# Halving one weight rounding per boundary and reworking the first tile, the norm offset, the end and one bank in a three-block transformer kernel

## The reference

```python
# first block, twice
x = x + 0.5 * norm(swiglu(norm(x), gate, up, down))           # width 2816
x = x + norm(concat(retention, gated_delta)(norm(x)) @ w_out) # 4 + 4 heads of 128, both directions
x = x + norm(cross_attention(norm(x), norm(mem)) @ xattn_o)   # 4 heads of 256, memory of 256 rows
x = x + 0.5 * norm(swiglu(norm(x), gate, up, down))
# second block, once
h = norm(x)
mixed = gate0 * (mamba2(h) @ w_ssm_out) + gate1 * (dilated_attention(h) @ w_att_out)
x = x + mixed @ w_mix_out
x = x + swiglu(norm(x), gate, up, down)
out = norm(x)

def norm(x, w):  # RMS norm over the 1024 columns
    return x * rsqrt(mean(x * x) + 1e-6) * w
```

## Time and profile before

| | |
|---|---|
| median of 3 runs | 1930.05 us (1928.93 to 1930.11) |
| the profiled execution | 1928.99 us, its span 1927.2 us |
| PE busy | 1910.8 us (99%), 11287 matmuls |
| POOL busy | 1544.8 us (80%) |
| ACT busy | 1087.2 us (56%) |
| DVE busy | 708.3 us (37%) |
| idle time of POOL's subtractions, until ACT's `whi` came | 332.0 us |
| chain that ended last | PE 94%, ACT 3%, DVE 2% |
| mean granted TensorE clock | 0.997 |

### The profile page before, as it was taken

How to read it: one execution, slowest core, us unless ns; L and a number is a source line. 1 busy time by engine, 2 the same in 40 slices (tenths; PEclk the granted TensorE clock), 3 DMA queues, 4 the chain that set the end, 5 groups by cost and what they waited for, 6 DMA issues and landing times.

```text
span 1927.2 us, 28342 instructions
## 1 busy us (share of the span) xinstructions
PE 1910.8 (99%) x11287; PEld 1683.6 (87%) x11287; DVE 708.3 (37%) x1406; ACT 1087.2 (56%) x1458; POOL 1544.8 (80%) x1227
## 2 busy tenths in 40 slices
PE   9999999999999999999999999999999999999998
PEld 7888899988888888889999888888999998888887
DVE  2221767521211222138574231113676632122112
ACT  6645674456644575456734665446666667545443
POOL 6998786666899799979776759997767787888995
PEclk9999999999999999999999999999999999999999
DMA  8554543143655565555323536555443444545552
GB/s 320 191 193 173 203 148 132 49 179 124 221 195 192 183 228 198 189 183 195 134 88 110 193 113 217 182 192 212 152 158 136 153 154 153 178 177 202 197 187 98
DMA packets 48661, 331.50 MB, mean 172 GB/s; under 512 B 5393, under 2 KB 6289, under 8 KB 10514
## 3 DMA queue, kind: packets, MB, share of 16 engines
q1 hardware_dynamic: 44208, 314.61, 45.1%
q10 hardware_dynamic: 4322, 15.09, 2.2%
HBM read 328.63 MB, written 1.05 MB: 171 GB/s over the span
## 4 chain that ended last, share of the span: by engine, by line
PE 94%; ACT 3%; DVE 2%; ACTq 1%; issue 0%; DVEq 0%; DMA 0%
PE bank L1942 20%; PE bank L1911 16%; PE bank L1912 16%; PE bank L1913 16%; PE bank L1946 10%; ACT arena L417 1%; PE bank L2050 1%; PE bank L2074 1%; PE bank L2386 1%; PE bank L2402 1%; PE bank L2016 1%; PE bank L2052 1%; PE bank L2508 1%; PE bank L2647 1%; PE bank L2487 1%
## 5 line engine op out<-in xcount | busy, mean ns | idle before, releaser
L390 POOL TENSOR_TENSOR wlo<-raw,whi 128x512 fp32r<-128x512 f32 x1184 | 1501.8, 1310 | 332.6 <-ACT whi L417 332.0
L417 ACT ACTIVATE whi<-raw 128x2048 fp32r<-128x2048 f32 (+1 forms) x299 | 568.1, 1902 | 192.0 <-PE bank L1913 156.6
L417 ACT ACTIVATE arena<-bank 128x512 f32<-128x512 f32 (+4 forms) x389 | 210.8, 552 | 439.8 <-PE bank L1946 266.4
L1942 PE MATMUL bank<-uT,whi 128*128 128x512 f32 x1632 | 408.2, 392 | 0.0
L1942 PEld LDWEIGHTS bank<-uT,whi 128*128 128x128 f32 x1632 | 296.3, 189 | 55.0
L1946 PEld LDWEIGHTS bank<-uT,wlo 128*128 128x128 f32 x1632 | 222.6, 190 | 15.9
L1946 PE MATMUL bank<-uT,wlo 128*128 128x256 f32 x1632 | 227.5, 282 | 0.0
L1911 PE MATMUL bank<-uT,whi 128*128 128x256 f32 x768 | 222.6, 290 | 0.3 <-DVE memT L1221 0.3
L1912 PE MATMUL bank<-uT,whi 128*128 128x256 f32 x768 | 217.1, 283 | 0.0
L1913 PE MATMUL bank<-uT,wlo 128*128 128x256 f32 x768 | 217.1, 283 | 0.0
L1911 PE MATMUL bank<-whi,uT 128*128 128x512 f32 (+1 forms) x416 | 160.8, 387 | 0.0
(11 more groups left out here) (315 smaller groups left out, 2698.6 us busy)
## 6 DMA issues: line engine op xcount, KB each, us to landing
raw<-in_w SPq DMA_DIRECT2D x295, 1024.0 KB, 4.8
rows<-in_rows ACTq DMA_DIRECT2D x22, 512.0 KB, 4.9
raw<-in_w SPq DMA_DIRECT2D x4, 512.0 KB, 7.2
arena<-in_mem ACTq DMA_DIRECT2D x2, 1024.0 KB, 9.5
x<-in_x SPq DMA_DIRECT2D x2, 512.0 KB, 5.4
out<-x SPq DMA_DIRECT2D x2, 512.0 KB, 2.7
arena<-in_amask ACTq DMA_DIRECT2D x1, 576.0 KB, 6.1
cst<-in_cst SPq DMA_DIRECT2D x1, 468.0 KB, 10.9
```

Source lines behind the costliest of these rows:

```text
L390: r = pool.tensor_tensor(wlo[n % LAND][:, k], raw[n % LAND][:, k], whi[n % RING][:, k].bitcast(F32), ALU.subtract)
L417: return act.activation(o, i, f, **k)
L1942: pe.matmul(both, w[0][:, c], parts[:, :, k, :], start=start and k == 0, stop=False)
```

## The change

Six edits, made together:

- **Half rounding.** In `boundary`, unit B is rounded in two activations of 128x1024, one before `u_hi(1)` and one behind it. `w_hi` is counted up by the second.
- **Norm offset.** The offset sum/n + eps of every pre-norm is made by DVE (`pre_bias`, a tensor_scalar of 128x1) and not by ACT. ACT tells with `pre_sum` that the first half's sum is there and waits for `norm_dve` before the root.
- **First tile.** PE multiplies the cleared tile four more times behind the first two matmuls of unit 0, and twice more ahead of unit 1.
- **Memory bank.** The fourth part of y goes to bank 4 and not to bank 6 again, behind a wait for `m_ready`; ACT and DVE copy it right behind the other three.
- **End.** Tile 0's final scaling is moved up and cut in halves. Tile 1's is shared: POOL multiplies half 0 by the weights and ACT scales it by the reciprocal, DVE does both for half 1. SP stores tile 1 from `ub`.
- **Semaphores.** `cst_in`, `pos_in` and `lvl_in` become one, `tables_in`, waited for at 48; `cleared` becomes `pool_side`.

```diff
@@ -345,17 +345,18 @@
                 if n == 0:
                     sp.dma_start(x[:, 1, :], a["x"][:, 1, :]).then_inc(sems["x_in1"], 16)
             sp.dma_start(raw[2][:], a["w"][2]).then_inc(sems["raw_landed2"], 16)
-            sp.dma_start(cst[:, P:], a["cst"][:, P:]).then_inc(sems["cst_in"], 16)
-            sp.dma_start(posi, a["pos"].to_broadcast((P, SEQ))).then_inc(sems["pos_in"], 16)
...
-                sp.dma_start(out[0, t * P:(t + 1) * P, :], x[:, t, :]).then_inc(sems["stored"], 16)
+            sp.wait_ge(sems["out_ready"], 2)
+            sp.dma_start(out[0, 0:P, :], x[:, 0, :]).then_inc(sems["stored"], 16)
+            sp.wait_ge(sems["out_ready"], 4)
+            sp.dma_start(out[0, P:SEQ, :], ub[:, 1, :]).then_inc(sems["stored"], 16)
             sp.wait_ge(sems["stored"], 16 * NT)
 
...
@@ -406,6 +407,10 @@
                     masks_of(LAST_LEVEL)
                 if n - 20 in mix0:
                     score_masks()
+            r = N_ROWS - 1
+            pool.wait_ge(sems[f"row_landed{r % 3}"], 16 * (r // 3 + 1))
+            pool.wait_ge(sems["x_part2"], 4 * DEPTH + 2)
+            pool.tensor_tensor(ub[:, 1, 0:512], x[:, 1, 0:512], rows[:, r % 3, 0:512], ALU.mult).then_inc(sems["pool_side"], 1)
 
 
         @block.scalar
@@ -429,6 +434,19 @@
                     fn(whi[s][:], raw[b][:], AF.Copy).then_inc(sems["w_hi"], 1)
                     state["split"] += 1
 
+            def split_half(half):
+
+                n = state["split"]
+                s, b = n % RING, n % LAND
+                k = slice(half * UNIT // 2, (half + 1) * UNIT // 2)
+                if half == 0:
+                    act.wait_ge(sems[f"raw_landed{b}"], p.count(f"raw_landed{b}", 16))
+                    act.wait_ge(sems["unit_done"], p.value("unit_done", n - RING + 1))
+                r = fn(whi[s][:, k], raw[b][:, k], AF.Copy)
+                if half:
+                    r.then_inc(sems["w_hi"], 1)
+                    state["split"] += 1
+
             def split_to(u):
 
                 split(max(0, min(u + RING, N_UNITS) - state["split"]))
@@ -461,11 +479,15 @@
                            accum_out=st[:, c0 + 2 * h + t:c0 + 2 * h + t + 1])
                     if done == "rms_post":
                         r.then_inc(sems["squared"], 1)
-                    act.drain()
-                    if h == 0:
+                    d = act.drain()
+                    if h == 0 and done == "rms_pre":
+                        d.then_inc(sems["pre_sum"], 1)
+                    elif h == 0:
                         fn(st[:, c0 + 4 + t:c0 + 5 + t], st[:, c0 + t:c0 + t + 1], AF.Identity, scale=1.0 / n, bias=eps)
                 if parts[-1] == 0:
                     return
+                if done == "rms_pre":
+                    act.wait_ge(sems["norm_dve"], p.count("norm_dve"))
                 fn(st[:, c0 + 6 + t:c0 + 7 + t], st[:, c0 + 2 + t:c0 + 3 + t], AF.Sqrt, scale=1.0 / n,
                    bias=st[:, c0 + 4 + t:c0 + 5 + t]).then_inc(sems[done], 1)
 
@@ -520,8 +542,9 @@
                 if half:
                     post_root(1, half, last, (1,))
                 pre_root(1)
-                split()
+                split_half(0)
                 u_hi(1)
+                split_half(1)
                 split()
 
             def hi_parts(dst, banks, n0=0):
@@ -973,14 +996,12 @@
                 fn(Ssb, bank[0][:, :], AF.Copy).then_inc(sems["act_read0"], 1)
                 for hp in range(4):
                     if hp == 2 and g == 2:
-                        hi_parts(mT, (6, 1, 7))
+                        hi_parts(mT, (6, 1, 7, 4))
                     if hp == 2 and g < SSM_GROUPS - 1:
                         conv_in(g + 1, 1)
                     elif hp == 2:
                         act.wait_ge(sems["unit_done"], p.value("unit_done", att0 + 2))
                         split_to(att0 + 2)
-                    if hp == 2 and g == 2:
-                        hi_parts(mT, (6,), 3)
                     act.wait_ge(sems["ssm_arg"], p.count("ssm_arg"))
                     fn(bank[4 + hp % 2][:, :], bank[4 + hp % 2][:, :], AF.Exp).then_inc(sems["ssm_decay"], 1)
                 if g < SSM_GROUPS - 1:
@@ -1112,6 +1133,9 @@
             ffn(b2 + 60)
             for t in range(NT):
                 pre_root(t)
+            act.wait_ge(sems["pool_side"], DEPTH + 1)
+            act.wait_ge(sems["norm_dve"], p.count("norm_dve"))
+            fn(ub[:, 1, 0:512], ub[:, 1, 0:512], AF.Copy, scale=st[:, 55:56]).then_inc(sems["out_ready"], 1)
 
 
         @block.vector
@@ -1126,8 +1150,15 @@
                 dve.wait_ge(sems[f"row_landed{r % 3}"], p.count(f"row_landed{r % 3}", 16))
                 return rows[:, r % 3, :]
 
+            def pre_bias(t):
+
+                dve.wait_ge(sems["pre_sum"], p.count("pre_sum"))
+                ts(st[:, 52 + t:53 + t], st[:, 48 + t:49 + t], 1.0 / D, EPS, ALU.mult, ALU.add)\
+                    .then_inc(sems["norm_dve"], 1)
+
             def pre_scale(t, w):
 
+                pre_bias(t)
                 r = st[:, 54 + t:55 + t]
                 dve.wait_ge(sems["rms_pre"], p.count("rms_pre"))
                 dve.reciprocal(r, r)
...
@@ -1881,15 +1911,23 @@
             u_lo(1, 1)
             ffn()
             w = use_row()
-            for t in range(NT):
-                row_add(t, 0, N_UNITS - 1)
-                row_add(t, 1, N_UNITS - 1)
-            for t in range(NT):
-                r = st[:, 54 + t:55 + t]
-                dve.wait_ge(sems["rms_pre"], p.count("rms_pre"))
-                dve.reciprocal(r, r)
-                dve.drain()
-                stt(x[:, t, :], x[:, t, :], r, w, ALU.mult, ALU.mult).then_inc(sems["out_ready"], 1)
+            row_add(0, 0, N_UNITS - 1)
+            row_add(0, 1, N_UNITS - 1)
+            pre_bias(0)
+            dve.wait_ge(sems["rms_pre"], p.count("rms_pre"))
+            dve.reciprocal(st[:, 54:55], st[:, 54:55])
+            dve.drain()
+            stt(x[:, 0, 0:512], x[:, 0, 0:512], st[:, 54:55], w[:, 0:512], ALU.mult, ALU.mult).then_inc(sems["out_ready"], 1)
+            row_add(1, 0, N_UNITS - 1)
+            stt(x[:, 0, 512:], x[:, 0, 512:], st[:, 54:55], w[:, 512:], ALU.mult, ALU.mult).then_inc(sems["out_ready"], 1)
+            row_add(1, 1, N_UNITS - 1)
+            pre_bias(1)
+            dve.drain()
+            tt(ub[:, 1, 512:], x[:, 1, 512:], w[:, 512:], ALU.mult)
+            dve.wait_ge(sems["rms_pre"], p.count("rms_pre"))
+            dve.reciprocal(st[:, 55:56], st[:, 55:56]).then_inc(sems["norm_dve"], 1)
+            dve.drain()
+            ts(ub[:, 1, 512:], ub[:, 1, 512:], st[:, 55:56], None, ALU.mult).then_inc(sems["out_ready"], 1)
 
 
         @block.tensor
@@ -2086,11 +2124,13 @@
                     pe.wait_ge(sems["u_hi"], p.count("u_hi"))
                     pe.wait_ge(sems["w_hi_half"], 1)
                     part_phase(wa, 0, a, 0, 0, (0, 1))
+                    idle_products(4)
                     pe.wait_ge(sems["w_hi"], 1)
                     part_phase(wa, 0, a, 0, 0, (2, 3))
                     pe.wait_ge(sems["first_lo"], 1)
                     part_phase(wa, 1, a, 0, 0, (0, 1))
                     lo_phase(wa, a, 0, 0, True)
+                    idle_products(2)
                     pe.wait_ge(sems["u_hi"], p.count("u_hi"))
                     pe.wait_ge(sems["w_hi_half"], 2)
                     part_phase(wb, 0, a, 0, 1, (0, 1))
...
@@ -2634,7 +2674,8 @@
                 proj_T(conv_bank[1], "conv" if g < SSM_GROUPS - 1 else "dve", uT, False,
                        (lambda: y_part((6, 1, 7), 0)) if g == 2 else None)
                 if g == 2:
-                    y_part((6,), 3)
+                    pe.wait_ge(sems["m_ready"], p.n["m_ready"] + 1)
+                    y_part((4,), 3)
                 acquire(0, "dve")
                 pe.matmul(bank[0][:, :], cout2[g % 2][:, 1, P:2 * P], Ssb, start=True, stop=True).then_inc(sems["dve_bank0"], 1)
                 acquire(1, "dve")
```

25 lines of the change are left out of this document (12 added, 13 removed).

## The result

| | before | changed |
|---|---|---|
| profiled execution | 1928.99 us, span 1927.2 | 1935.30 us, span 1933.5 |
| median of 5 runs | 1929.92 us (1928.93 to 1930.11) | 1937.64 us (1935.30 to 1939.58) |

The ratio is 1.0037 (95% interval 1.0026 to 1.0048), so the changed kernel is slower by about 0.4%. The prediction, 1931.8 us with a range of 1927.5 to 1934.5, was wrong. The runs of the changed kernel also lie further apart, 4.3 us against 1.2, and its profiled execution is the fastest of them.

The account below looks back on a forecast made before the run. PE was taken to bound the kernel, busy 1910.8 of 1927.2 us. 1928.99 + 3.5 (boundaries) - 0.5 (first tile) - 0.65 (bank) - 0.6 (end) = 1930.7 us; with 1.06 for the median, 1931.8, range 1927.5 to 1934.5.

Parts of the forecast that it names:

- Half rounding at the four boundaries: Near 212, 436, 873 and 1097 us: PE waits for unit B's late low part, +4.3 us net of offset gains.
- The boundary into the second block: Like the feed-forward boundaries: small products and a pause come before B's low part, so the 0.20 us gain stays.
- 0.1 us was added: First boundary's form: unit B lies more beside DVE's long operations, which slow POOL's pieces; 0.1 us more.
- First tile: Start of the kernel: extra products fill PE's gap and may bring the full clock sooner; -0.5 us.
- The bounds (-1.2 to +1.0): First tile: gain of 1.2 us if the clock were full throughout, loss up to 1.0 if it rises at 14.8.
- Norm offset: Each boundary: small activation leaves ACT, so tile 1's transposes and `u_hi(1)` come 0.20 us earlier; waiting for `norm_dve` costs nothing.
- Bank: Fourth part of y: PE's waits of 0.67 and 0.31 us go, `row_sums(2)` waits 0.3 us; net -0.65.
- End: Last scaling shared between ACT and DVE ends near 1923.5 us, so the store starts earlier; -0.6 us.
- The whole delay: Rival: at all four places PE pays 1.98 us or more for the late low part; 1935.4 us, chance 0.10.

Follow-up runs that it names:

- b_half8: The kernel before with the half rounding at all boundaries but the one into the second block; 1936.41 us, ratio 1.0028.
- b_half206: The kernel before with the half rounding only at the boundary into the second block; 1934.52 us, ratio 1.0017.
- b_half206_psum: b_half206 with one input of DVE's 128x32 multiply first copied to PSUM, ahead of the copy that frees bank 0; 1932.10 us, ratio 1.0005.
- b_idle: The kernel before with the six extra products in the first tile alone; 1930.43 us, ratio 0.9997.
- b_bank: The kernel before with only bank 4 for the fourth part of y; 1929.23 us, ratio 0.9994.
- b_half: The kernel before with the half rounding alone, at all boundaries; 1940.76 us, ratio 1.0054.
- a_noidle: The changed kernel without the six extra products in the first tile; 1936.88 us, ratio 1.0033 to the kernel before.
- a_psum: The changed kernel with one input of DVE's 128x32 multiply copied to PSUM, ahead of the copy freeing bank 0; 1934.82 us, ratio 1.0022 to the kernel before.
- b_norm: The kernel before with only the offset of the pre-norms moved to DVE; 1929.55 us, ratio 0.9996.

## Why the prediction was wrong, point by point

- **Half rounding at the four boundaries (+4.3).** Right in place and mechanism, a little small. POOL's idle time before unit B was forecast at 5.8 to 6 us and is 6.2 to 6.3; PE's waits are 1.0 to 1.3 us. With the gains ahead of them the four places cost 1.30 + 1.08 + 1.60 + 1.04 = 5.0 us; b_half8, without the gain of the offset, measured 5.2 in the median and 6.0 within a group.
- **The boundary into the second block (-0.2): this is the step that failed.** The prediction said that it "is alike" the feed-forward ones, because PE has small products and a pause before it needs B's low part. That is true, and PE never waits for `wlo` there (b_half206). But the step asked only whether PE waits for POOL. The delay moved POOL's row of subtractions against two DVE operations on which PE does wait, 14 and 32 us later: +0.9 at 1359 us in all eight profiles with the half rounding there, and at 1377.7 us up to 2.5 more, with up to 1.6 for the clock. b_half206 shows that this boundary alone costs 3.3 us, and b_half206_psum that some 2.3 of them are the multiply's wait. That it is the position of the subtractions, and not POOL's lateness or its lost pauses as such, is read from the start and end times of the seventeen profiles; no run moved POOL's row by a chosen amount.
- **A rule was weighed for one side only.** By rows of POOL, 0.1 us was added for what DVE does to it; what POOL does to DVE was not asked. The trace shows 3.7 us with two SBUF inputs and 0.19 with one in PSUM. The Trainium skill's GPSIMD Engine Reference (8. Key points) names DVE instructions with two SBUF inputs among those in contention with POOL; the trace agrees, 3.7 us against 0.19.
- **First tile (-0.5).** +1.98 in the profiles compared, but the products are not its cause: within a group b_idle gains 0.6 to 0.8 us, as forecast. The bounds (-1.2 to +1.0) were set within one start; what moved was the start itself, which the row products show ahead of any edit. The prediction named that no row shows a second start, and it should have widened the range for it: before's profile had the early kind, as its other four runs did by their times, and the changed kernel's profile had the late one. That these two profiles differ in kind is chance, as far as the runs show. The Trainium skill, TensorE: Matmul & The Clock Gate (Part 1: The HAM clock gate), lets the moment of the change vary with the start, and the profiles agree: tile 1 between 18.2 and 21.0 us without the products.
- **Norm offset.** Right: 0.13 to 0.43 us against 0.20 at each boundary. It costs 0.33 to 0.37 at 988 us, where the prediction had nothing, and at the end it would have cost 1.0 us if the end had not been reworked with it, which the prediction had not seen.
- **Bank (-0.65).** Right in the sum: -0.61 (b_bank -0.62). Gains and cost were both larger than forecast, the new cost 0.85 and not 0.3, and it came at the products of L2688 and not at `row_sums(2)`.
- **End (-0.6).** Right: from the start of PE's last product to the end 7.06 us became 6.34.
- **Rivals.** The whole delay (1935.4, 0.10) came nearest to the time, but not for its reason: the delay did not come through whole, PE paid 1.0 to 1.3 us at each place.

So the 7.7 us are, against a forecast of +1.75 on the same base: 0.9 more at the boundaries, 0.9 at 1359 us, 0.4 at 988, 2.5 for the start, which differs between executions, and in most executions the multiply and the clock behind it, up to 4. Left open: why the multiply gets through at the next end of a subtraction in some executions and at the third in others (in the changed kernel's profile it met POOL at the same point as in b_half and took 1.18 us), and why the clock fell behind the wait in b_half and a_noidle but not in b_half206. How often the changed kernel meets the slow multiply was not seen, since its one profile lacks it; what speaks for "most" is that four of its five runs took 1936.08 to 1939.58 us, where a_psum's eleven end at 1935.29 and are 2.8 us faster in the median. The step at 988 us belongs to the norm offset, since b_norm alone has it (+0.33); what makes it was not followed up.

No kernel tried has a better ratio than the changed one without the half rounding: 1927.84 and 1927.97 us on two chips, 0.17 to 0.18% under the kernel before.

## What to carry to other kernels

When an edit delays an engine that has slack, ask two things. Does someone wait for it now? And what runs beside it, and where will its instructions then stand against that? Here a shift of POOL's row against them by a fraction of one subtraction went with short DVE operations that took 0.9 to 2.7 us longer. So follow the delay until the pause that absorbs it, and look at every short operation there that the bounding engine waits for. And before a term is built on the first microseconds of a profile, look whether the part that no edit touches runs alike in a second execution.

## What the runs showed of the hardware

- A DVE multiply of 128x32 with two SBUF inputs took 1.01 to 1.18 us beside POOL's subtractions when it got through at the next end of one, and 3.68 to 3.72 when it waited for the third, which was the last of a row of 28 (which of the two counts, the profiles do not tell); with one input in PSUM, 0.19 us beside the same row.
- A DVE scalar_tensor_tensor of 128x64 with both inputs in SBUF took 0.24 to 0.29 us when it started up to 0.21 us ahead of the end of a subtraction, and 1.17 to 1.24 when it started 0.09 to 0.16 us behind one (seventeen profiles).
- A wait of 2.25 us on PE was followed by a stretch at the lower clock that cost 1.6 us (b_half; a_noidle likewise, after 2.23), while one of 2.20 us in b_half206 was not.
- The granted clock of the first products, which no kernel changed, differs between executions by enough to move tile 1 by about 2 us, and the times of most kernels split into two groups by it.
- A window's clock is 1.00 where the trace has no record of it yet; products of 0.43 to 0.48 us in it, where 0.23 is usual, show that it was half.
